# Slot table by one-hot products on TensorE, with the shared expert, the accumulator's store and one group of transposes in another order

## The reference

```python
x = layer_norm(ALPHA * x + token_mixer(x), ...)      # RG-LRU and S5 branches
# mixture of experts: 64 experts of width 256, 8 picked per token, one shared
scores = sigmoid(x @ router_w)
masked = where(group is among the best 4 of 8, scores + router_bias, -inf)
expert_idx = top_k(masked, 8)
gate = 2.5 * scores[expert_idx] / sum(scores[expert_idx])
y  = (silu(x @ ws_gate) * (x @ ws_up)) @ ws_down      # shared expert
y += sum over picked e of gate_e * ((silu(x @ wg_e) * (x @ wu_e)) @ wd_e)
ple = sigmoid(x @ ple_gate_w + ple_gate_b) * (p @ ple_w)
x = layer_norm(ALPHA * x + y + ple, ...)
```

## Time and profile before

| | us |
|---|---|
| median of 3 runs | 1528.13 |
| fastest and slowest | 1526.51 and 1529.31 |
| profiled execution, its own time | 1527.41 |
| its span | 1525.6 |
| TensorE busy | 1408.9 (92%) |
| VectorE busy | 867.1 (57%) |
| ScalarE busy | 608.1 (40%) |
| GpSimd busy | 464.6 (30%) |
| mean granted clock of TensorE | 0.964 |

### The profile page before, as it was taken

One profiled execution on the slowest core, in us unless ns is written; L12 is line 12 of the kernel. 1 busy time (PEld: TensorE's weight loads), 2 busy tenths in 40 slices (PEclk: granted clock), 3 DMA queues, 4 the chain that ended last, 5 costly groups with the idle time before them and its releaser, 6 DMA issues.

```text
span 1525.6 us, 18528 instructions
## 1 busy us (share of the span) xinstructions
PE 1408.9 (92%) x6293; PEld 931.9 (61%) x6293; DVE 867.1 (57%) x1240; ACT 608.1 (40%) x850; POOL 464.6 (30%) x415
## 2 busy tenths in 40 slices
PE   7979898998999999999957799999999999999990
PEld 4456777675788888555423466666666666666650
DVE  4598778785500100344712667766677667666655
ACT  3114654537422222010001555555555555555540
POOL 1012535333544443000261233222222222223322
PEclk8999999999899999999978899999999999999996
DMA  8035343434233334730045699999999999999953
GB/s 245 0 110 79 76 71 73 80 64 103 62 96 98 90 103 165 300 138 1 1 168 211 225 355 362 355 366 359 366 359 357 363 371 367 362 365 357 365 173 124
DMA packets 141491, 315.97 MB, mean 207 GB/s; under 512 B 18898, under 2 KB 100514, under 8 KB 116160
## 3 DMA queue, kind: packets, MB, share of 16 engines
q1 hardware_dynamic: 125984, 281.50, 53.3%
q0 software_dynamic: 15456, 33.79, 9.4%
HBM read 297.35 MB, written 34.65 MB: 218 GB/s over the span
## 4 chain that ended last, share of the span: by engine, by line
PE 75%; DVE 6%; DMA 6%; issue 4%; DVEq 2%; another core or an unknown queue 2%; POOL 2%; ACT 1%; POOLq 1%; SPq 0%; ACTq 0%
PE bank L701 14%; PE bank L703 14%; PE bank L702 14%; PE bank L1059 13%; PE bank L708 5%; PE bank L933 4%; PE bank L919 4%; PE bank L735 3%; DMA gate_up<-moe_w_up_in 3%; DVE arena L1335 3%; DVEq L1332 2%; DMA acc_dram<-arena 2%; PE bank L834 1%; POOLq L589 1%
## 5 line engine op out<-in xcount | busy, mean ns | idle before, releaser
L1335 DVE TENSOR_TENSOR gate_up_low<-gate_up,gate_up_high 128x1024 fp32r<-128x1024 f32 x256 | 296.5, 1220 | 98.4 <-ACT gate_up_high L1116 97.6
L1116 ACT ACTIVATE arena<-bank 96x512 f32<-96x512 f32 (+5 forms) x248 | 131.6, 554 | 413.2 <-PE bank L1059 138.4
L1116 ACT ACTIVATE gate_up_high<-gate_up 128x1024 fp32r<-128x1024 f32 x256 | 249.5, 1047 | 58.3 <-DMA gate_up<-moe_w_up_in 42.8
L1059 PE MATMUL bank<-down,arena 128*96 128x512 f32 x512 | 230.4, 592 | 1.0 <-DVE arena L1848 1.0
L1335 DVE TENSOR_TENSOR arena<-arena 128x512 f32<-128x512 f32 (+10 forms) x286 | 205.9, 752 | 18.9 <-ACT arena L1116 4.7
L701 PE MATMUL bank<-gate_up_high,rows_high 128*96 128x512 f32 x512 | 207.1, 404 | 5.4 <-DVE rows_low L1335 5.4
L703 PE MATMUL bank<-gate_up_high,rows_low 128*96 128x512 f32 x512 | 203.6, 398 | 0.0
L702 PE MATMUL bank<-gate_up_low,rows_high 128*96 128x512 f32 x512 | 202.0, 394 | 0.0
L708 PEld LDWEIGHTS bank<-arena 96*128 96x128 f32 (+4 forms) x1001 | 128.1, 186 | 66.4 <-issue 48.7
L554 POOL TENSOR_TENSOR wb_low<-arena,wb_high 128x1024 fp32r<-128x1024 f32 (+1 forms) x40 | 110.0, 2753 | 147.4 <-ACT wb_high L1116 147.4
L708 PE MATMUL bank<-arena 96*128 96x96 f32 (+4 forms) x1001 | 127.8, 267 | 18.6 <-DVE arena L1341 9.4
(11 more groups left out here) (150 smaller groups left out, 2161.8 us busy)
## 6 DMA issues: line engine op xcount, KB each, us to landing
gate_up<-moe_w_gate_in SPq DMA_DIRECT2D x64, 1024.0 KB
gate_up<-moe_w_up_in SPq DMA_DIRECT2D x64, 1024.0 KB
down<-moe_w_down_in SPq DMA_DIRECT2D x64, 1024.0 KB
arena<-w_in_in SPq DMA_DIRECT2D x40, 512.0 KB, 4.0
arena<-w_glu_in SPq DMA_DIRECT2D x16, 512.0 KB, 3.9
arena<-w_lru_out_in SPq DMA_DIRECT2D x8, 768.0 KB, 4.9
arena<-x_in SPq DMA_DIRECT2D x8, 512.0 KB, 5.2
arena<-w_in_in SPq DMA_DIRECT2D x2, 2048.0 KB, 11.7
```

The costliest lines, as they stand in the source:

```text
L1059: last = mm(banks[5 + hf][0:SL, :], heT[u % 2][:, k], dn[u % 4][:, k, hs], start=(k == 0), stop=(k == 1))
L1116: return nc.scalar.activation(out_, in_, func, **kw)
L1335: return V_.tensor_tensor(out_, a, b_, op)
```

## The change

The 32 indirect writes, the table in DRAM and the reading back go. In their place VectorE makes for each tile of tokens two sets of one-hot rows (`picks`): which of the 106 tiles a pick is in (8 x 106 columns), and which of the 96 places (8 x 96), once times the token number and once times the gate. TensorE multiplies them, 32 matmuls of 192 columns that add up in one bank (`slot_table`), and turns the result (`table_turn`); an empty slot comes out as token number 1024. The list of experts for overflow tiles becomes a one-column matmul instead of comparisons on one partition. GpSimd only clears the row buffers, behind `res_put`.

The order of the shared expert changes: products into banks 4, 5, 2 and 3, all four behind the last `ple_value`, then the turns and output products one after another, with adds and semaphores by half tile. The accumulator is stored in four transfers of 0.5 MB, each behind its own adds; the gate and up weights of expert 3 are loaded ahead of them and its down weights behind them. The powers' transposes stand one `u_proj` earlier.

```diff
             sp.wait_ge(S["ple_put"], 2 * TT)
             sp.wait_ge(S["ple_val"], TT)
             load_expert(0, 0, s_wgu[0], s_wdn[0])
-            sp.wait_ge(S["slot_ready"], 1)
+            sp.wait_ge(S["table_put"], 1)
             sp.wait_ge(S["ple_done"], TT)
             sp.wait_ge(S["x1_stored"], 16 * TT)
             load_expert(1, 1, s_wgu[1], s_wdn[1])
             sp.wait_ge(S["sh_put"], TT)
             load_expert(2, 2, s_wgu[2], s_wdn[2])
-            sp.wait_ge(S["sh_y_put"], TT)
-            load_expert(3, 3, s_wgu[3], s_wdn[3])
-            sp.wait_ge(S["sh_done"], TT)
-            sp.dma_start(acc_dram[0:T, :].rearrange("(t p) d -> p t d", p=P), acc).then_inc(S["acc_stored"], 16)
+            load_in(3, 3, s_wgu[3])
+            for t in range(TT):
+                sp.wait_ge(S["sh_done"], 2 * t + 2)
+                sp.dma_start(acc_dram[t * P:(t + 1) * P, :], acc[:, t, :]).then_inc(S["acc_stored"], 16)
+            sp.wait_ge(S["sh_y_put"], 2 * TT)
+            load_down(3, 3, s_wdn[3])
...
-            pool.wait_ge(S["padded"], 16)
             pool.wait_ge(S["res_put"], 2 * TT)
-            pool.wait_ge(S["slot_ready"], 1)
-            nc.gpsimd.memset(xg_all, 0.0)
-            pool.drain()
-            for t in range(TT):
-                for k in range(K):
-                    nc.gpsimd.indirect_dma_start(
-                        out=slot_dram, out_offset=bass.IndirectOffsetOnAxis(ap=sloti[:, t, k:k + 1].bitcast(u32), axis=0),
-                        in_=pairs[:, t, k, :], in_offset=None).then_inc(S["tok_stored"], 16)
-            pool.wait_ge(S["tok_stored"], 16 * TT * K)
-            nc.gpsimd.dma_start(slotR.rearrange("p s v -> p (s v)"), slot_dram.rearrange("(n s) v -> n (s v)", s=SL)
-                                ).then_inc(S["tok_loaded"], 16)
-            pool.wait_ge(S["tok_loaded"], 16)
-            nc.gpsimd.tensor_copy(slotD.rearrange("n (m q) v -> n m q v", m=NDMA),
-                                  slotR.rearrange("n (q m) v -> n m q v", m=NDMA)).then_inc(S["slots_dealt"], 1)
+            nc.gpsimd.memset(xg_all, 0.0).then_inc(S["rows_zeroed"], 1)
...
             pool.wait_ge(S["x1_stored"], 16 * TT)
-            pool.wait_ge(S["ple_done"], TT)
             for u in range(4):
                 gather(u, u, u)
-            pool.wait_ge(S["acc_stored"], 16)
+            pool.wait_ge(S["acc_stored"], 16 * TT)
...
-            for n in range(1, TT + 2):
+            for n in range(1, TT + 1):
                 u_proj(n)
...
-            for n in range(TT + 2, 2 * TT):
+            for n in range(TT + 1, 2 * TT):
...
+            def slot_table():
+                for t in range(TT):
+                    pe.wait_ge(S["picks_ready"], t + 1)
+                    for k in range(K):
+                        last = mm(banks[6][0:NT, 0:2 * SL], in_tile[t][:, k, :], at_slot[t][:, :, k, :],
+                                  start=(t == 0 and k == 0), stop=(t == TT - 1 and k == K - 1))
+                mm(banks[7][0:1, 400:448], texcol, ident[:, 0:48], start=True, stop=True).then_inc(S["table_put"], 1)
+            def table_turn():
+                pe.wait_ge(S["table_kept"], 1)
+                for v in range(2):
+                    last = tp(banks[7][0:SL, v * P:v * P + NT], slotD[:, v * SL:(v + 1) * SL], NT)
+                last.then_inc(S["tokT_put"], 1)
...
             ple_gate(0)
+            ranks()
             ple_gate(1)
             ple_value(1)
-            pe.wait_ge(S["mask_ready"], 1)
-            for t in range(TT):
-                for s in range(t + 1):
-                    mm(banks[7][:, t * E:(t + 1) * E], strict if s == t else ones, mask[:, s, :], start=(s == 0), stop=(s == t))
-            for s in range(TT):
-                last = mm(banks[7][:, TT * E:(TT + 1) * E], ones, mask[:, s, :], start=(s == 0), stop=(s == TT - 1))
-            last.then_inc(S["router_put"], 1)
             pe.wait_ge(S["shared_loaded"], 48)
             sh_in(0)
-            for t in (2, 3):
-                ple_gate(t)
-                ple_value(t)
-            def sh_out(t):
+            ple_gate(2)
+            slot_table()
+            ple_value(2)
+            table_turn()
+            ple_gate(3)
+            ple_value(3)
+            sh_in(1)
+            pe.wait_ge(S["ple_done"], TT)
+            sh_in(2)
+            sh_in(3)
...
+            def sh_turn(t):
                 pe.wait_ge(S["sh_hid"], t + 1)
+                need(pe, "sh_hT", t - 1)
                 hv = hdn[t % 2].rearrange("p (d k) -> p k d", k=2)
                 for k in range(2):
+                    last = tp(banks[4 + t % 2][:, k * P:(k + 1) * P], hv[:, k, :], P)
                 last.then_inc(S["sh_hT_put"], 1)
+            def sh_out(t):
                 pe.wait_ge(S["sh_hT"], t + 1)
+                if t == 0:
+                    pe.wait_ge(S["idx_ready"], 1)
                 for hf in range(2):
+                    need(pe, "sh_done", 2 * (t - 1) + hf + 1)
...
-            pe.wait_ge(S["idx_ready"], 1)
-            pe.wait_ge(S["sh_done"], TT)
+            sh_turn(0)
+            sh_turn(1)
+            sh_out(0)
             x_turn(0, 0)
-            for u in range(0, 5):
+            sh_out(1)
+            sh_turn(2)
+            sh_out(2)
+            sh_turn(3)
+            sh_out(3)
+            expert(0, 0)
+            pe.wait_ge(S["sh_done"], 2 * TT)
...
+            sh_silu(0)
+            sh_silu(1)
+            act.wait_ge(S["table_put"], 1)
             gate_up_high(0, 0)
+            sh_silu(2)
             rows_high(0, 0)
-            act.wait_ge(S["acc_stored"], 16)
+            sh_silu(3)
+            act.wait_ge(S["acc_stored"], 16 * TT)
...
+            def picks(t):
+                tt(in_tile[t], bc(iota_n, 1, K), bc(tilef[:, t, :], 2, NT), ALU.is_equal)
+                tt(at_slot[t][:, 1], bc(iota_s, 1, K), bc(inf_[:, t, :], 2, SL), ALU.is_equal)
+                d()
+                ts(at_slot[t][:, 0], at_slot[t][:, 1], tok[:, t:t + 1], None, ALU.mult)
+                d()
+                tt(at_slot[t][:, 1], at_slot[t][:, 1], bc(gate[:, t, :], 2, SL), ALU.mult).then_inc(S["picks_ready"], 1)
+            for t in range(TT):
+                tt(eqt[:, t], bc(iota_e, 1, K), bc(idx8f[:, t, :], 2, E), ALU.is_equal)
+            ple_bias(0, 0)
+            d()
+            for t in range(TT):
+                tt(eqp[:, t], eqt[:, t], bc(score[:, t, :], 1, K), ALU.mult)
+            ple_bias(0, 1)
+            d()
+            V_.tensor_reduce(gate, eqp, AX, ALU.add)
+            d()
+            V_.tensor_reduce(gsc, gate, AX, ALU.add)
+            d()
+            V_.reciprocal(gsc, gsc)
+            d()
+            for t in range(TT):
+                ts(gate[:, t, :], gate[:, t, :], gsc[:, t:t + 1], SCALE, ALU.mult, ALU.mult)
...
+            ts(tilef, slotf, 1.0 / SL, -(SL - 1) / (2.0 * SL), ALU.mult, ALU.add)
+            d()
+            ts(tilef, tilef, MAGIC, None, ALU.add)
+            d()
+            ts(tilef, tilef, -MAGIC, None, ALU.add)
+            d()
+            stt(inf_, tilef, -float(SL), slotf, ALU.mult, ALU.add)
+            d()
+            dve.wait_ge(S["rows_zeroed"], 1)
+            ple(0)
+            picks(0)
+            ple_bias(1, 0)
+            ple_bias(1, 1)
+            picks(1)
+            ple(1)
+            picks(2)
+            picks(3)
             ple_bias(2, 0)
-            for t in range(TT):
-                tt(eqp[:, t], eqt[:, t], bc(score[:, t, :], 1, K), ALU.mult)
-            d()
-            V_.tensor_reduce(gate, eqp, AX, ALU.add)
-            d()
-            V_.tensor_reduce(gsc, gate, AX, ALU.add)
-            d()
-            V_.reciprocal(gsc, gsc)
-            d()
-            for t in range(TT):
-                ts(pairs[:, t, :, 1], gate[:, t, :], gsc[:, t:t + 1], SCALE, ALU.mult, ALU.mult)
-            d()
-            dve.sem_inc(S["slot_ready"], 1)
+            ple_bias(2, 1)
+            dve.wait_ge(S["table_put"], 1)
+            ts(texpi[0:1, :].bitcast(i32), banks[7][0:1, 400:448], float(E - 1), None, ALU.min).then_inc(S["texp_ready"], 1)
+            V_.tensor_copy(slotD, banks[6][0:NT, 0:2 * SL]).then_inc(S["table_kept"], 1)
             ple(2)
+            dve.wait_ge(S["tokT_put"], 1)
+            V_.tensor_copy(gateT, banks[7][0:SL, P:P + NT])
+            ts(idxT.bitcast(i32), banks[7][0:SL, 0:NT], float(NOROW), None, ALU.add)
+            d()
+            dve.sem_inc(S["idx_ready"], 1)
+            ple_bias(3, 0)
+            ple_bias(3, 1)
...
+            sh_hid(0)
+            sh_hid(1)
             gate_up_low(0, 0)
+            sh_keep(0)
+            sh_hid(2)
+            sh_keep(1)
+            sh_hid(3)
+            sh_add(0)
             rows_low(0, 0)
+            sh_keep(2)
+            sh_add(1)
+            sh_keep(3)
+            sh_add(2)
+            sh_add(3)
```

More of the change, by code:

```diff
@@ L55 @@
 LEVELS = (T - 1) // SL
+NOROW = 2 * T
 BIG = 1e30
@@ L1738, in _ @@
             ts(repl, row, SL - 0.5, None, ALU.is_gt)
```

(6 more changed lines are left out.)

136 lines of the change are left out of this document (50 added, 86 removed).

## The result

The changed kernel takes 1506.59 us (median of 4 runs, 1504.88 to 1510.24), the kernel before 1527.32 beside it (4 runs, 1525.73 to 1529.31): ratio 0.9861, 95% interval 0.9842 to 0.9881, so 20.7 us less. Forecast was 1505, with 1500 to 1510 for the forecast case and 1496 to 1522 for all. The profiled execution is the slowest of the four, 1510.24 us with a span of 1508.5; it lost some 3 us in the first 36 us, where the first product of the u projection stands at 18.51 and takes 10.08 us (before: 17.57 and 8.86), and the next begins at 35.61 instead of 32.43. Such shifts come and go: over all profiles of this document the first gate product begins at 684.99 to 690.80 us in the five kernels without part 1 and at 679.47 to 683.27 in the nine with it.

The account below looks back on a forecast made before the run. TensorE was taken to bound the kernel, with the expert loop untouched, so gains ahead of it pass through: 7 us at the start plus 16.2 before expert 1 make 23.2, forecast 1505 us, range 1496 to 1522 (own case 1500 to 1510).

Parts of the forecast that it names:

- part 1: Start, u projection: powers' transposes one product earlier shorten TensorE's 7.91 us wait for x_low; gain 7 us, ends 0 and 8.4.
- The walk: TensorE from first gate product to gate-up of expert 0: 123.2 us of work plus 10.0 of waits, ending at 821.8.
- The weight loads: Slot table on TensorE: loads taken as hidden, 0.161 us a row, 10.3 us; by the skill page 16 us.
- Rival E: Slot table: 64 rows with unhidden weight loads at 0.62 us each, 29.4 us more, 1534; chance 0.03.
- The silent waits: Shared expert: unexplained waits of ScalarE's third silu (17.4 us) and VectorE's first add (5.0), left out as gone with the writes.
- rival A: Shared expert: silent waits come from a program place or expert-load burst, not the writes; 5 to 20 us, about 1517; chance 0.15.
- part 2: Gates to expert 0: TensorE's new order with the slot table, putting gate-up of expert 0 at 821.8.
- part 3: Ahead of expert 1: accumulator store split in four; gate-up of expert 1 at 835.2 against 851.42, gain 16.2 us.
- The store: Last accumulator quarter: lands 5.4 us after issue, like x stores of that size, at 828.0; ends 5.4 and 17.55.
- Rival B: Accumulator store: no shorter when split, as it queues behind expert loads; 12.2 us more, 1517; chance 0.08.
- Sum: Whole kernel: 7 + 16.2 = 23.2 us off 1527.41, giving 1504.2; median of runs 1505.

Follow-up runs that it names:

- a_fill: The kernel after with the first shared-in product ahead of value product 1 on TensorE: 1500.15 us, ratio 0.9820 to the kernel before.
- b_store: The kernel before with only the accumulator's store split in four and expert 3's gate and up loaded ahead: 1519.10 us, ratio 0.9949.
- b_paced: The kernel before with GpSimd waiting for each 8 indirect writes to land, instead of once after all 32: 1520.19 us, ratio 0.9939.
- a_paced: a_better with the slot table built by GpSimd's indirect writes, in groups of 8 and begun early, instead of on TensorE: 1480.97 us, ratio 0.9699.
- a_better: a_fill with hidden turns and silu moved up in the shared-out, and per-tile store waits for expert 1's high part: 1488.42 us, ratio 0.9744.
- a_writes: The kernel after with 32 indirect writes to an unread DRAM scratch put back on GpSimd: 1532.35 us, ratio 1.0037 to the kernel before.
- b_powers: The kernel before with only the powers' transposes moved one product of the u projection earlier: 1520.17 us, ratio 0.9948.
- b_few_writes: The kernel before with 4 indirect writes instead of 32, leaving out most of the expert sum: 1504.80 us, ratio 0.9846.

## Why the prediction was right

- **Part 1.** Forecast 7 us, with 1.4 more if the clock stays: it stays (1.00 in the window from 88 us), the wait is 1.04 us, and alone the part gives 7.9. Right, and nearer to its upper end of 8.4.
- **The walk.** From the first gate product to gate-up 0 it forecast 133.2 us; the trace has 820.65 - 683.27 = 137.4. The waits came as worked out: 4.74 for value 1 (forecast 5.0), 0.28 + 2.38 + 1.20 + 1.20 = 5.1 in the shared-out (5.0). The table took 10.56 us (10.3), and the picks were covered. What the walk left out is the granted clock behind these waits, though the prediction had just used it at x_low: value 1 took 2.75 us more at a clock of 0.58 than without the wait (3.60 in a_fill), shared-out 1 took 1.7 more at 0.68 than its neighbours. Together that is 4.45 us, all of the 4.2 that were missing.
- **The weight loads.** The table's rows took 0.165 us each, as the row of 512 columns had given (0.161). By the Trainium skill, "TensorE: Matmul & The Clock Gate", section "Part 3: Packing small matmuls", its weight loads would not be hidden, and the prediction's estimate from that was 16 us. The trace does not agree with it: 10.56 us. Rival E is out.
- **The silent waits** were left out of the walk as gone, although all that spoke for it was that the writes ran at the same time. That was a bet (rival A had 0.15), and it came out: they are gone, and for the suspected cause, as the runs with few, with paced and with added writes show. By what means the writes hold up an engine stays open. Rival A (a place in the programs, or the burst) falls for ScalarE, and holds for VectorE's 5 us only together with the writes. The prediction never asked what part 2 gives by itself. It gives nearly nothing (1 us, within 3.5): the gain comes from parts 1 and 3, and from what part 2 does for part 3.
- **The store.** Forecast landing 5.4 us, measured 2.92; gate-up 1 follows gate-up 0 by 11.5 us instead of 13.4. The 5.4 of the x stores is a median of four, and the kernel before shows them one by one: 18.3 and 7.8 us for the first two, issued while the queues moved over 400 GB/s, and 2.6 and 3.0 for the last two. The last accumulator store of after is like the last two, and reading them singly would have given 2.6 to 3.0. Here the estimate of 3.2 from the Trainium skill's "DMA: Bandwidth & Descriptors", section "Anatomy of one DMA", was the nearer one, though that section describes transfers issued by GpSimd and these are SyncE's; for the store behind 3 MB it gives 6.8 against the 15 to 17.6 measured. Rival B was right in part in b_store (12.07 us), where the loads ahead are issued later. The four x stores, in order of time:
```profile
x_dram<-arena SPq DMA_DIRECT2D x1, 512.0 KB, 18.3
...
x_dram<-arena SPq DMA_DIRECT2D x1, 512.0 KB, 7.8
...
x_dram<-arena SPq DMA_DIRECT2D x1, 512.0 KB, 2.6
...
x_dram<-arena SPq DMA_DIRECT2D x1, 512.0 KB, 3.0
```
- **Sum.** Parts 2 and 3 were to bring 16.2 us and brought 14.0: 4.2 lost in the walk, 1.9 won behind it. Part 1 brought some 1 us more than forecast, and gate-up of expert 1 lost 1.1 us to the lower clock: 23.2 - 4.2 + 1.9 + 0.9 - 1.1 = 20.7, the measured gain (part 1's share is known to 2.5 us only). The mechanism held, but that the time came within 1.6 us of the forecast is partly luck: the lower clock cost some 5.5 us that no term allowed for, and errors of the other sign gave 2.8 back. Without those the time would have been about 1509.4, still inside the range.

## What to carry to other kernels

When an engine stands idle and nothing in its program explains it, look at what else is in flight, and test that by itself: one added pause per 8 indirect writes took away the same waits as a table rebuilt on TensorE (b_paced), though it brought another one of 10.45 us. With an earlier start, and on top of the other parts and the better order, it came out 6.6 us ahead of the table (a_paced against a_better, in the stretches). Price a store by the loads issued just ahead of it, not by its size alone, and look at equal transfers one by one before taking their median. And price a TensorE wait with the clock that follows it: here gaps of 2.38 and 4.74 us cost another 1.7 and 2.75.

## What was not expected of the hardware

- 32 indirect writes issued 1.27 us apart hold up TensorE, VectorE and ScalarE, from 18 us in (a_writes) or by 28 us in (before), until 4.3 to 4.7 us behind the last; TensorE itself was held up only in a_writes. Four writes, or groups of 8 with a landing between them, do not. GpSimd waited 1.41 us for such a landing with 1 GB/s on the queues (b_paced, 792.90 to 794.40) and up to 5.55 beside 6 MB of loads.
- Behind a wait of 2.38 us on TensorE the granted clock was 0.68 (5.37 us for a product of 3.67); behind waits of 1.20 and 1.04 us it stayed up. A wait of 1.83 us in the same place went both ways: the product behind it took 5.40 us at 0.68 in b_powers and b_few_writes, and 3.70 at 1.00 in before.
- A store of 2 MB just behind 3 MB took 15.05 to 17.55 us in five kernels, 24.22 behind 9 MB; one of 0.5 MB took 2.92 us with 5 MB of loads issued from 24 us ahead, 4.39 with them from 17 us ahead and 12.07 from 12 us ahead.
